# Recurrent block of a two-block network on one core: one tap of its convolution moved to ScalarE, and two late projections computed from weights in high and low parts

## What is computed

```python
def rglru_mixer(h, w_in, conv_w, conv_b, w_a, b_a, w_x, b_x, lam, w_out):
    proj = h @ w_in                                # 1024 x 2048
    xb, yb = jnp.split(proj, 2, axis=-1)
    y_gate = jax.nn.gelu(yb)
    xp = jnp.pad(xb, ((0, 0), (CONV_LEFT, CONV_W - 1 - CONV_LEFT), (0, 0)))
    xc = sum(xp[:, j:j + S] * conv_w[j] for j in range(CONV_W)) + conv_b
    def direction(d, reverse):
        r = jax.nn.sigmoid(block_diag_linear(xc, w_a[d], b_a[d]))
        ig = jax.nn.sigmoid(block_diag_linear(xc, w_x[d], b_x[d]))
        log_a = -LRU_C * r * jax.nn.softplus(-lam[d])
        a = jnp.exp(log_a)
        mult = jnp.sqrt(-jnp.expm1(2.0 * log_a))
        _, hs = lax.associative_scan(lin_combine, (a, mult * ig * xc), axis=1, reverse=reverse)
        return hs
    hsum = direction(0, False) + direction(1, True)
    return (hsum * y_gate) @ w_out
```

## Time and profile before

| | us |
|---|---|
| median of 3 runs | 2950.66 (2950.29 to 2952.08) |
| the profiled execution | 2949.61 |
| its span, first to last instruction | 2947.9 |
| TensorE busy in the span | 2923.3 |
| recurrent block, input projections begun to output projection begun | 2036.1 to 2120.5 |

### The profile page before, as it was taken

The page is one execution under the profiler, slowest core; times in us unless marked ns, Lnnn a source line. Parts: engine busy times, 40 slices in busy tenths (PEclk is TensorE's granted clock), DMA queues, the critical chain, the costliest instruction groups (busy, mean ns, idle before and its releaser), DMA issues.

```text
span 2947.9 us, 52959 instructions
## 1 busy us (share of the span) xinstructions
PE 2923.3 (99%) x18318; PEld 2610.5 (89%) x18318; DVE 2266.7 (77%) x4250; ACT 1551.5 (53%) x2599; POOL 675.7 (23%) x514
## 2 busy tenths in 40 slices
PE   9999999999999999999999999999999999999998
PEld 8887888888788899899999988888799999988887
DVE  8886888788777689778878866667678887966666
ACT  5446543545555465655554455555655555455554
POOL 0120111010100000017787011110006777211110
PEclk9999999999999999999999999999999999999999
DMA  8773786876237654157776467786347776467775
GB/s 344 283 291 115 259 300 246 296 289 236 86 129 239 217 198 132 72 171 186 187 189 153 160 216 217 232 287 230 141 157 187 187 189 167 147 204 217 217 217 173
DMA packets 201303, 601.61 MB, mean 204 GB/s; under 512 B 53073, under 2 KB 85969, under 8 KB 173905
## 3 DMA queue, kind: packets, MB, share of 16 engines
q1 hardware_dynamic: 142176, 521.19, 52.4%
q0 software_dynamic: 58272, 75.66, 10.9%
q10 hardware_dynamic: 720, 3.00, 0.2%
HBM read 581.81 MB, written 17.96 MB: 203 GB/s over the span
## 4 chain that ended last, share of the span: by engine, by line
PE 89%; DVE 3%; ACT 2%; issue 0%; DMA 0%; DVEq 0%; SPq 0%; ACTq 0%
PE turn L397 48%; PE gather L397 39%; ACT arena L1637 1%; PE turn L1080 0%; ACT hT L1637 0%; DVE arena L2654 0%; DVE arena L2649 0%; DVE arena L2702 0%; ACT expert_src_high L1637 0%; DVE keyed L2321 0%; DVE arena L2669 0%; ACT L1637 0%; DVE arena L2318 0%; DMA ring<-stream 0%; PE gather L799 0%
## 5 line engine op out<-in xcount | busy, mean ns | idle before, releaser
L1637 ACT ACTIVATE dense<-ring 128x1024 fp32r<-128x1024 f32 x542 | 573.3, 1058 | 372.3 <-PE gather L397 343.4
L3021 DVE TENSOR_TENSOR ring_low<-ring,dense 128x1024 fp32r<-128x1024 f32 x542 | 660.9, 1220 | 128.6 <-ACT dense L1637 126.9
L397 PE MATMUL turn<-expert_src_high,ring_low 128*128 128x256 f32 x2600 | 725.0, 279 | 0.0
L3349 POOL DMA_INDIRECT gates<-ring x256 | 476.7, 1862 | 761.3 <-DVE ring L3125 628.7
L397 PE MATMUL turn<-expert_src_high,dense 128*128 128x256 f32 x2288 | 645.5, 282 | 0.3
L397 PE MATMUL turn<-expert_src_low,dense 128*128 128x256 f32 x2288 | 636.4, 279 | 0.0
L397 PE MATMUL gather<-dense 128*128 128x512 f32 x2048 | 631.7, 389 | 0.0
L397 PEld LDWEIGHTS turn<-expert_src_high,ring_low 128*128 128x128 f32 x2600 | 488.7, 188 | 0.0
L397 PE MATMUL turn<-rounded 128*128 128x512 f32 x1392 | 480.0, 390 | 0.6 <-DVE rounded L2462 0.6
L397 PEld LDWEIGHTS gather<-dense 128*128 128x128 f32 x2048 | 384.4, 188 | 79.9
L397 PEld LDWEIGHTS turn<-expert_src_high,dense 128*128 128x128 f32 x2288 | 430.3, 188 | 0.7 <-DVE ring_low L3021 0.7
(11 more groups left out here) (316 smaller groups left out, 4154.2 us busy)
## 6 DMA issues: line engine op xcount, KB each, us to landing
ring<-tiles_in SPq DMA_DIRECT2D x544, 512.0 KB
ring<-stream SPq DMA_DIRECT2D x204, 1024.0 KB, 5.6
arena<-ada_in POOLq DMA_DIRECT2D x96, 512.0 KB, 4.5
gates<-keyed SPq DMA_DIRECT2D x16, 1024.0 KB, 7.8
ring<-gates POOLq DMA_DIRECT2D x128, 128.0 KB, 3.4
arena<-tables_in POOLq DMA_DIRECT2D x6, 1024.0 KB, 8.1
gates<-ring POOLq DMA_INDIRECT x256
arena<-keys_in SPq DMA_DIRECT2D x2, 1024.0 KB, 7.7
```

The source lines that it names most:

```text
L397: return nc.tensor.matmul(out, lhsT, rhs, start=start, stop=stop, skip_group_check=True)
L1637: return nc.scalar.activation(out, in_, func, **kw)
L3021: V.tensor_tensor(tile_words(t, ring_low).bitcast(R32), tile_words(t), tile_high[:, t % AHEAD, :], ALU.subtract).then_inc(S("tile_low"), 1)
L3349: pool.indirect_dma_start(gates_flat[l], bass.IndirectOffsetOnAxis(offsets[:, h, c:c + 1], 0), weights[:, 1, h, c:c + 1], None, bounds_che ...
```

## The change

Three things are changed. The tap j = 2 with the bias becomes an activation on ScalarE, straight from the PSUM bank, ahead of the copy of each pair; VectorE adds the other three taps to it. The late projections 9 and 10 become split ones: their four high halves are made by ScalarE behind gate groups 2 and 3 of gate piece 0 and behind groups 1 and 2 of gate piece 1, their low halves by VectorE behind the convolution and between the two power steps of the first direction. And the low part of the input moves to a region that stays free until the late projections, while the new homes lie over the second direction's `lru_h` and over the convolution's input; the second direction's first scans therefore wait until piece 9 is done. Piece 11 stays native, and the decays stay on ScalarE where they were.

```diff
--- before.py
+++ after.py
@@ -452,7 +452,7 @@
         PARTED = {
             "mla": [(1, 1), (2, 0), (2, 1)],
             "nsa": [(i, b) for i in range(2, 5) for b in range(2)],
-            "lru": [(1, 1)] + [(i, b) for i in range(2, 5) for b in range(2)]}
+            "lru": [(1, 1)] + [(i, b) for i in (2, 3, 4, 9, 10) for b in range(2)]}
         PARTED_BEFORE = {"mla": 1, "nsa": 3, "lru": 6}
 
         def part_base(stage):
@@ -770,9 +770,9 @@
             "mla": homes("mla", aligned(qh_at), 2) + homes("mla_last", aligned(vh_at), 1),
             "nsa": homes("nsa_first", aligned(vh_at), 1) + homes("nsa", aligned(phase), 3)
             + homes("nsa_last", aligned(biased_at) + KC * T, 2),
-            "lru": homes("lru", lru_a_at, 7)}
+            "lru": homes("lru", lru_a_at, 7) + homes("lru_late", lru_h_at + KC * T, 2) + homes("lru_last", 0, 2)}
         PARTED_LOW = {"mla": over("mla_low", aligned(probs_at), KC, T),
-                      "nsa": over("nsa_low", aligned(biased_at), KC, T), "lru": over("lru_source_low", lru_h_at, KC, T)}
+                      "nsa": over("nsa_low", aligned(biased_at), KC, T), "lru": over("lru_source_low", LATE + KC * T, KC, T)}
 
         @block.tensor
         def _(pe):
@@ -1424,6 +1424,11 @@
 
                 def late(j):
                     q = q0 + LATE_PIECES[j]
+                    if j < 2:
+                        for b in range(2):
+                            last = parted_half("lru", Y[j], q, 9 + j, b)
+                        last.then_inc(piece_done, 1)
+                        return
                     arrive(pe, q)
                     project_pair(q, Y[j], hT).then_inc(piece_done, 1)
 
@@ -2065,6 +2070,10 @@
                     act.wait_ge(piece_done, q0 + i + 1)
                     b4 = i % 4
                     if i < 4:
+                        for f in range(2):
+                            k = 2 * b4 + f
+                            run(conv[:, k, :], B[b4][:, f * T:(f + 1) * T], ACT.Identity,
+                                bias=param("conv_b", k), scale=param("conv_w", KC * CONV_LEFT + k))
                         run(conv_in[:, 2 * b4:2 * b4 + 2, CONV_LEFT:CONV_LEFT + T], B[b4][:, :], ACT.Copy)\
                             .then_inc(S("lru_taken"), 1)
                         if i < 2:
@@ -2073,6 +2082,8 @@
                         run(y_gate[:, 2 * b4:2 * b4 + 2, :], B[b4][:, :], ACT.Gelu_apprx_tanh)\
                             .then_inc(S("lru_taken"), 1)
                 q0 = piece_base("lru_gates")
+
+                LATE_HIGHS = {(0, 2): (9, 0), (0, 3): (9, 1), (1, 1): (10, 0), (1, 2): (10, 1)}
 
                 def gates(i, between=None):
 
@@ -2092,6 +2103,8 @@
                             at = KC * (i // 2) + k
                             run(dst[:, k, :], B[n % 4][:, f * T:(f + 1) * T], ACT.Tanh,
                                 bias=sp_t[:, 8 + i % 2, at:at + 1], scale=0.5).then_inc(S("lru_taken"), 1)
+                        if (i, j) in LATE_HIGHS:
+                            parted_high("lru", [LATE_HIGHS[i, j]])
 
                 def decays(d):
                     def chunk(k):
@@ -2960,20 +2973,18 @@
                     if pair in (1, 2):
                         parted_low("lru", PARTED["lru"][1 + 2 * pair:3 + 2 * pair])
                     dve.wait_ge(S("lru_taken"), pair + 1)
-                    for j in range(CONV_W):
+                    for j in (0, 1, 3):
                         for k in (2 * pair, 2 * pair + 1):
                             src = conv_in[:, k, j:j + T]
                             w = param("conv_w", KC * j + k)
-                            if j == 0:
-                                chain.add(V.tensor_scalar(conv[:, k, :], src, w, param("conv_b", k),
-                                                          ALU.mult, ALU.add))
-                                continue
-                            chain.wait(chain.n - 1 if j < CONV_W - 1 or k == 2 * pair else chain.n)
+                            if j > 0:
+                                chain.wait(chain.n - 1 if j < CONV_W - 1 or k == 2 * pair else chain.n)
                             ins = V.scalar_tensor_tensor(conv[:, k, :], src, w, conv[:, k, :], ALU.mult, ALU.add)
                             if j < CONV_W - 1:
                                 chain.add(ins)
                             else:
                                 ins.then_inc(S("conv_ready"), 1)
+                parted_low("lru", [(9, 0), (9, 1)])
                 for d in range(2):
                     for c in range(2):
 
@@ -2984,6 +2995,8 @@
                         then(V.tensor_tensor(z[:, sl, :], a, a, ALU.mult))
                         V.scalar_tensor_tensor(tau, z[:, sl, :], 1.0, tau, ALU.add, ALU.mult)\
                             .then_inc(S("lru_power"), 1)
+                        if (d, c) == (0, 0):
+                            parted_low("lru", [(10, 0), (10, 1)])
                     dve.wait_ge(S("lru_taken"), 5 + 16 * (d + 1))
                     for c in range(2):
                         sl = slice(4 * c, 4 * c + 4)
@@ -2992,6 +3005,8 @@
                     for c in range(2):
                         sl = slice(4 * c, 4 * c + 4)
                         dve.wait_ge(S("lru_root"), 2 * d + c + 1)
+                        if (d, c) == (1, 0):
+                            dve.wait_ge(piece_done, piece_base("lru_gates") + LATE_PIECES[0] + 1)
                         chain.wait()
                         then(V.tensor_tensor(lru_m[d][:, sl, :], lru_m[d][:, sl, :], lru_i[d][:, sl, :], ALU.mult))
                         for k in range(4 * c, 4 * c + 4):
```

## The result

The changed kernel took 2953.91 us in the median of 22 runs (2952.26 to 2955.97), the kernel before 2949.99 us in 22 runs on the same chip (2949.08 to 2952.08). The ratio is 1.0014, with a 95% interval of 1.0007 to 1.0020: slower by 3.9 us, within 0.2%. Forecast were 2953.3 us, with 2951.0 to 2956.5 as the range, and "within 0.2%" as the likeliest case. The profiled execution of the changed kernel took 2955.97 us, the longest of its 22 runs, so its rows show more loss than the median has. That difference is the second half of this story.

The account below looks back on a forecast made before the run. The prediction took ScalarE, then VectorE, then TensorE to bound the second half of the recurrent block. Its terms, 0 + 2.65 + 0 + 0 us on a median of 2950.66, gave 2953.3 us, range 2951.0 to 2956.5.

Parts of the forecast that it names:

- What bounds the block: Second half of the recurrent block: bound by ScalarE first, VectorE behind it, TensorE last.
- Part 1, the tap: Convolution: unshifted tap on ScalarE is covered on both engines, 0 us; without that cover 4.0 us.
- Part 2, the copies: Gate groups: four high-half copies on ScalarE, the first hidden, then 0.75, 0.95 and 0.95, sum 2.65 us; bounds 1.9 and 3.9.
- Part 3, the low halves: Behind the convolution and between power steps: four VectorE subtractions fit in idle time, 0 us; 2.3 us if cover went.
- Part 4, TensorE: Late projections ahead of the output projection: split saves 2.33 us, which goes into a TensorE wait of some 3.4 us.
- Hidden copies: Rival, ScalarE in the gate stretch: its high-half copies cost nothing, 2950.7 us; chance 0.06.
- a saving that counts: Rival, ahead of the output projection: TensorE's shorter projections gain time, 2951.0 us, or 2948.3 with hidden copies; chance 0.03.
- more uncovered copies: Rival, ScalarE: all four copies uncovered, 3.9 us, late piece 10 or taps adding up to 4.0: 2954.6 to 2958.6; chance 0.07.
- The clock falls in the new wait: Rival, output projection: TensorE's clock halves after the 3.4 us wait, up to 7.1 us more, up to 2960.4; chance 0.06.
- The sum: Whole kernel: 0 + 2.65 + 0 + 0 = +2.65 us, median 2953.3 us, 0.09% more.
- at clock 1.00: Expected sign ahead of the output projection: about 3.4 us of TensorE idle with the granted clock still 1.00.
- a clock of 0.50 behind the wait: Sign of a wrong forecast: TensorE's clock at its lower level after the wait ahead of the output projection.

Follow-up runs that it names:

- e6_highs_vector: Changed kernel with the four high halves of pieces 9 and 10 made by VectorE instead of ScalarE: 2951.62 us, ratio 1.0006 to the kernel before.
- e3b_fewer_fillers: Changed kernel with 14 unused filler products on TensorE in the wait ahead of the output projection: 2952.73 us, ratio 1.0009 to the kernel before.
- e2_late_alone: Changed kernel with all four convolution taps back on VectorE, so only the split late projections: 2954.35 us, ratio 1.0014 to the kernel before.
- e10_delay_two: Kernel before with two added VectorE passes of 128x1024, results unused, ahead of the mixed channels: median 2954.25 us, ratio 1.0016.
- e4_mix_early: Changed kernel with the first two channel pairs mixed behind the first half of the second direction's scans: 2952.26 us, ratio 1.0007 to the kernel before.
- e1_tap_alone: Kernel before with only the unshifted convolution tap moved to ScalarE, late projections native: 2950.04 us, ratio 1.0000.
- e3_fillers: Changed kernel with 24 unused filler products on TensorE in the wait ahead of the output projection: 2954.24 us, ratio 1.0014 to the kernel before.

## Why the prediction was right, and where it was not

- **What bounds the block.** As put: ScalarE, then VectorE, then TensorE. The copies' removal brought the start of the output products back (e6_highs_vector) although the late projections stayed split.
- **Part 1, the tap: 0.** Right: 0.00 in both columns of the table. VectorE's convolution ended at 2066.9, or 2066.1 on the times of before, forecast 2066.2.
- **Part 2, the copies: 0 + 0.75 + 0.95 + 0.95 = 2.65.** Measured 0 + 0.74 + 0.94 + 0.94 = 2.62 at the last gate group, and 2.66 at the output products. The block from the end of the input projections took 2124.00 - 2068.57 = 55.43 us, forecast 55.4.
- **Part 3, the low halves: 0, with 0.8 us to spare.** Right: they were 0.74 us early.
- **Part 4, TensorE.** The saving was forecast at 2.33 and measured at 2.5, the wait at 3.4 and 3.61. That it would go into the wait is shown by e6_highs_vector. The step that the sum lacks is here: what the longer wait does to the clock was put at nothing.
- **The rivals.** Hidden copies, a saving that counts, more uncovered copies, a late load: none came true. *The clock falls in the new wait* did, and I gave it 0.06. The mechanism and the condition were stated as they turned out. Two sizes were off. The chance was too small: I read the tolerance from one fall, 4.4 us after the last matmul of the program, as if it were a fixed delay of which 3.4 us fell short. Six profiles now show falls 2.3, 2.4, 2.6, 3.3, 3.6 and 4.9 us after TensorE began to stand still. And the price, "up to 7.1 us", was too large: the low level ended before the 16 products did. The profiles show 1.5, 1.7 and 2.8 us, and in the median of the change it is 3.92 - 2.65 = 1.3 us.
- **The sum.** 2.65 forecast, 3.92 measured; the missing term is this 1.3. The runs of the changed kernel stand in three groups, 6 at 2952.3 to 2952.8, 8 at 2953.6 to 2954.6 and 8 at 2955.0 to 2956.0. The lowest is where e3b_fewer_fillers lies, whose clock never falls, and the profiled run with 2.78 us of clock loss is in the highest. The mean granted clock of each run, which is on record to three places, fits: 0.999 in all 6 of the lowest group, 0.998 in all 8 of the highest, and either in the middle one. So the groups look like no fall, a short low stretch and a long one; but where the clock was low is known for the profiled run alone, and a fall elsewhere, as near the start of e2_late_alone, can't be told apart from it.

The claim "at clock 1.00" in what would show it was wrong, and one of the signs named there for being wrong, a clock of 0.50 behind the wait, is what came. The range was said to leave this case out; that the time lies in it all the same is luck, since the price turned out small. So is a part of the closeness: the forecast of 2953.3 stood on a median of 3 runs, 2950.66, where 22 runs gave 2949.99. This 0.67 us too much and the 1.27 us too little in the sum partly cancel, and 0.6 us are left.

**The moment of the fall.** The profiles show falls 2.4, 3.3, 3.6 and 4.9 us after the beginning of waits of nearly one length, 3.54 to 3.61 us. The Trainium skill, "TensorE: Matmul & The Clock Gate", Part 1 "The HAM clock gate", says that the chip's interval of observation runs freely, so that the moment of a change varies between runs of one kernel; the falls at 2.4 and 3.6 us after the beginning of a wait of 3.61 us agree, though in two kernels.

## What to carry to other kernels

Price a copy by the gap in which it stands: four equal copies cost 0, 0.74, 0.94 and 0.94 us, and moved to an idle engine they cost nothing. Before TensorE's work is shortened, find out who releases its next step: the same split was worth nothing while VectorE set that point, and 2.6 us once VectorE's results came earlier. And count a new wait of TensorE as a possible loss of clock behind it, in some executions and not in others: here all six profiles with a wait of 2.1 to 3.6 us had a fall behind it, at a price of 1.5 to 2.8 us where the 16 products show it. The waits of 1.64 us ahead of the gates had none in five profiles, but near the start of e2_late_alone one of 1.58 us had, so there is no safe length to be read from these runs. Put such a price into the sum, or widen the range for it.

## What the runs showed of the hardware

- TensorE's clock can fall after TensorE has begun to work again: 1.3 us later in e10_delay_two, 0.5 us in e4_mix_early, where the wait had been only 2.13 us. A wait of 1.1 us had none behind it in the profiles of the kernel before and of e1_tap_alone. Once low, the clock stayed so for 3.4 us behind five of these waits and for 6.8 us in the changed kernel and near the start of e2_late_alone. The runs of the six kernels with a fall behind the wait span 1.9 to 5.8 us, without the one of 5914.58 us, those of the five experiments without a fall 0.8 to 1.8 us; those of the kernel before span 3.0 us beside the changed kernel, by a single run at 2952.08.
- VectorE's copy of 128x1024 into the high format took 0.69 us, ScalarE's 1.05 (after the change), and VectorE's subtraction of the same size 1.23. The Trainium skill, "VectorE: DVE Perf Modes", section "What auto-detection actually checks", says that an operation with one source in SBUF can take two elements a cycle where one with two sources of 32 bits can't; the two rows agree, and it makes VectorE the cheaper place for such copies where it has time.
- A float32 matmul of 128x128 by 128 columns is two instructions and cost 0.23 us (5.52 us for 24, e3_fillers).
